# The combine stage: one row of three tiles weighted on ScalarE, four tiles normed from the residual on ScalarE and GpSimd

## The chip, the cores and the metric

The kernel runs on one core of a Trainium2 chip. Its time is the device time of one execution, in microseconds. Before the change three runs took 1245.3, 1250.42 and 1256.1 us, a median of 1250.42 us.

## The reference, cut to what matters

The program is one step of a decoder layer: a mixer, a norm, a mixture of experts, and a last norm. Only the last lines are touched here:

```python
y = lax.map(expert_block, (xb, block_e)).reshape(P, D)
out = jnp.zeros((N + 1, D), jnp.float32).at[buf_tok].add(y.astype(jnp.float32) * buf_w[:, None])
...
ff = moe(h2.reshape(B * T, D), ...)
x = layer_norm(ALPHA * x + (1 + g2) * ff, ln_g_l[1], ln_b_l[1])
```

Each token has two experts, so its `ff` is the sum of two rows of `y`, each times its weight. With r = ALPHA * x + (1 + g2) * ff, the norm is (r - mean) * rstd * ln_g + ln_b over 1024 columns. There are 1024 prompt tokens (8 tiles of 128 rows) and 64 sample tokens (tile 8, 64 rows).

## The kernel before, in words

`block_combine` is the last of the kernel's blocks. Everything in it is float32. The tiles go in order, 0 to 8, and each engine runs an order written out by hand, with semaphores between the engines.

- **GpSimd's queue** first issues 18 indirect gathers (L2759), two per tile, that fetch both expert rows of every token from the DRAM tensor `y_d` into `yy[i][0]` and `yy[i][1]`. Only then does it issue the output of tiles 0 to 7 (L2766). Such an output adds the tile to `o_y_p`, which was filled with ln_b long before, so ln_b needs no instruction in the prompt tiles.
- **ScalarE** first makes diagonal matrices of the weights for the tiles that TensorE sums (L2774), then for each tile two small scalings of the row sum (L2786, L2787), the squares with their sum (L2789) and the square root (L2792). After the statistics of tile i it scales tile i - 1 by rstd (L2780, the function `scale`), which frees its output to be sent.
- **TensorE** forms the weighted sum of both rows in PSUM (L2750) for the tiles from `ON_DVE` on, with four pairs of banks in turn.
- **VectorE** runs `residual(i)` and then `normed(i - 1)`. `residual` forms the weighted sum itself for the tiles below `ON_DVE` (L2810, L2811), multiplies by g2 (L2817) and adds ALPHA * x with the row's sum (L2821; the row's sum comes out in a short read of the accumulator). `normed` forms (r - mean) * ln_g into `nrm` (L2831) and takes the reciprocal (L2837); for the sample tile it also takes a reciprocal (L2839) and adds ln_b (L2840), after which SyncE sends it (L2859).

There are two buffers for the residual (`acc`) and three for the normed tile (`nrm`): `normed(i)` waits with `done[i % 3]` until the output of tile i - 3 has landed.

Of the kernel before, what the change touches and what calls it, by code (L numbers as in the profile page):

```python
# [26 lines left out]
ALU, ACT, AX = mybir.AluOpType, mybir.ActivationFunctionType, mybir.AxisListType  # L27
# [2683 lines left out]
def block_combine(c):  # L2711

    nc, t, sem = c.nc, c.t, c.sem
    RY = NT

    def part(n, count=1):
        return c.combine[:, D * n:D * (n + count)]

    yy = [[part(2 * s + k) for k in range(2)] for s in range(RY)]
    acc = [part(2 * RY + s) for s in range(2)]  # L2720
    nrm = [part(2 * RY + 2 + s) for s in range(3)]
    g2s = part(2 * RY + 5)
    x1 = c.raw[:, 0:NT * D].rearrange("p (i d) -> p i d", i=NT)
    lng2, lnb2, g2 = (c.raw[:, D * (NT + n):D * (NT + n + 1)] for n in range(3))
# [3 lines left out]
    st, eps, both = c.combine[:, o:o + 48], c.combine[:, o + 48:o + 49], c.combine[:, o + 49:o + 49 + NT]  # L2728
    shares = sem("y9_shares")
    diag = c.combine[:, o + 64:o + 64 + NT * 2 * P].rearrange("p (i k q) -> p i k q", i=NT, k=2)  # L2730
    n_ready, scaled, sample_out = sem("n9_ready"), sem("n9_scaled"), sem("y9_sample")
    y_in = [sem(f"y9_in{s}") for s in range(RY)]
    done = [sem(f"y9_out{s}") for s in range(3)]
    b_done, d_done, y_sum, g2_done, sum_ready, less_done, squared, var_ready, eps_set, link = (
        sem(n) for n in ("b9_done", "d9_done", "y9_sum", "g29_done", "m9_ready", "less9_done", "s9_squared", "v9_ready", "e9_set", "l9"))
    smp = NP_TILES
    ON_DVE = 2

    with nc.Block() as block:
        @block.tensor  # L2740
        def _(pe):
            for i in range(ON_DVE, NT):
                T = tile_rows(i)
                pe.wait_ge(d_done, i + 1 - ON_DVE)
                pe.wait_ge(y_in[i % RY], 32 * (i // RY + 1))
                if i >= 4 + ON_DVE:
                    pe.wait_ge(g2_done, i - 3)
                for n in range(2):
                    for k in range(2):
                        mm = pe.matmul(c.bank(2 * (i % 4) + n)[0:T, :], diag[0:T, i, k, 0:T],  # L2750
                                       yy[i % RY][k][0:T, 512 * n:512 * n + 512], start=(k == 0), stop=(k == 1))
                mm.then_inc(y_sum, 1)

        @block.gpsimd
        def _(pool):
            def fetch(i):
                T = tile_rows(i)
                for k in range(2):
                    pool.indirect_dma_start(yy[i % RY][k][0:T, :], None, c.y_d,  # L2759
                                            bass.IndirectOffsetOnAxis(ap=c.dest_y[0:T, i, k:k + 1], axis=0)).then_inc(y_in[i % RY], 16)  # L2760

            for i in range(RY):
                fetch(i)
            for i in range(smp):
                pool.wait_ge(scaled, i + 1)
                pool.dma_start(t["o_y_p"][0, i * P:(i + 1) * P, :], nrm[i % 3], accum_op=ALU.add).then_inc(done[i % 3], 16)  # L2766

        @block.scalar
        def _(act):
            act.wait_ge(shares, 1)  # L2770
            for i in range(ON_DVE, NT):
                T = tile_rows(i)
                for k in range(2):
                    a = act.activation(diag[0:T, i, k, :], c.ident[0:T, :], ACT.Identity, scale=c.xw[0:T, i, k:k + 1])  # L2774
                a.then_inc(d_done, 1)
            act.wait_ge(eps_set, 1)

            def scale(i):
                act.wait_ge(n_ready, i + 1)
                act.activation(nrm[i % 3], nrm[i % 3], ACT.Identity, scale=st[:, 24 * (i % 2) + 16:24 * (i % 2) + 17]).then_inc(scaled, 1)  # L2780

            for i in range(NT):
                T = tile_rows(i)
                q = st[0:T, 24 * (i % 2):24 * (i % 2) + 24]
                act.wait_ge(sum_ready, i + 1)
                act.activation(q[:, 8:9], q[:, 0:1], ACT.Identity, scale=-1.0 / (32 * D)).then_inc(less_done, 1)  # L2786
                act.activation(q[:, 4:5], q[:, 0:1], ACT.Identity, scale=-1.0 / D).then_inc(less_done, 1)  # L2787
                act.wait_ge(less_done, 2 * i + 1)
                act.activation(squares[0:T, :], acc[i % 2][0:T, :], ACT.Square, bias=q[:, 8:9], scale=1.0 / 32,  # L2789
                               accum_out=q[:, 12:13]).then_inc(squared, 1)  # L2790
                act.wait_ge(squared, i + 1)
                act.activation(q[:, 12:13], q[:, 12:13], ACT.Sqrt, bias=eps[0:T, :]).then_inc(var_ready, 1)  # L2792
                if i >= 1:
                    scale(i - 1)

        @block.vector
        def _(dve):
            links = [0]

            def linked(ins):  # L2800
                links[0] += 1
                ins.then_inc(link, 1)
                dve.wait_ge(link, links[0])

            def residual(i):
                T = tile_rows(i)
                ac = acc[i % 2][0:T, :]
                if i < ON_DVE:
                    dve.wait_ge(y_in[i], 32)
                    linked(dve.tensor_scalar(ac, yy[i][0][0:T, :], c.xw[0:T, i, 0:1], None, ALU.mult))  # L2810
                    linked(dve.scalar_tensor_tensor(out=ac, in0=yy[i][1][0:T, :], scalar=c.xw[0:T, i, 1:2], in1=ac,  # L2811
                                                    op0=ALU.mult, op1=ALU.add))
                    total = ac
                else:
                    dve.wait_ge(y_sum, i + 1 - ON_DVE)
                    total = c.psum[0:T, D * (i % 4):D * (i % 4) + D]
                dve.tensor_tensor(ac, total, (g2 if i < smp else g2s)[0:T, :], ALU.mult).then_inc(g2_done, 1)  # L2817
                dve.wait_ge(g2_done, i + 1)
                dve.wait_ge(c.x1_in[i], 32)
                q = st[0:T, 24 * (i % 2):24 * (i % 2) + 24]  # L2820
                dve.scalar_tensor_tensor(out=ac, in0=x1[0:T, i, :], scalar=ALPHA, in1=ac, op0=ALU.mult, op1=ALU.add,  # L2821
                                         accum_out=q[:, 0:1]).then_inc(sum_ready, 1)

            def normed(i):
                T = tile_rows(i)
                q = st[0:T, 24 * (i % 2):24 * (i % 2) + 24]
                out = nrm[i % 3][0:T, :]
                if i >= 3:
                    dve.wait_ge(done[i % 3], 16 * (i // 3))
                dve.wait_ge(less_done, 2 * i + 2)  # L2830
                linked(dve.scalar_tensor_tensor(out=out, in0=acc[i % 2][0:T, :], scalar=q[:, 4:5], in1=lng2[0:T, :],  # L2831
                                                op0=ALU.add, op1=ALU.mult))
                dve.wait_ge(var_ready, i + 1)
                if i < smp:
                    if i >= 2:
                        dve.wait_ge(scaled, i - 1)  # L2836
                    dve.reciprocal(q[:, 16:17], q[:, 12:13]).then_inc(n_ready, 1)  # L2837
                    return
                linked(dve.reciprocal(q[:, 16:17], q[:, 12:13]))  # L2839
                dve.scalar_tensor_tensor(out=out, in0=out, scalar=q[:, 16:17], in1=lnb2[0:T, :],  # L2840
                                         op0=ALU.mult, op1=ALU.add).then_inc(b_done, 1)

            dve.memset(eps, EPS).then_inc(eps_set, 1)
            linked(dve.tensor_tensor(both, c.xw[:, :, 0], c.xw[:, :, 1], ALU.add))
            linked(dve.reciprocal(both, both))
            dve.tensor_tensor(c.xw, c.xw, both.unsqueeze(2).to_broadcast([P, NT, 2]), ALU.mult).then_inc(shares, 1)
            dve.wait_ge(shares, 1)
            dve.wait_ge(c.v_in, 64)
            for i in range(NT):
                residual(i)  # L2850
                if i >= 1:
                    normed(i - 1)
            normed(smp)

        @block.sync
        def _(sp):
            sp.dma_start(g2s[0:NS, :], sample_rows(c, 5)).then_inc(c.v_in, 16)
            sp.wait_ge(b_done, 1)
            sp.dma_start(t["o_y_s"].rearrange("b j d -> (b j) d"), nrm[smp % 3][0:NS, :]).then_inc(sample_out, 16)  # L2859
            sp.wait_ge(c.out_done, c.out_total)  # L2860
            for s in range(3):
                sp.wait_ge(done[s], 16 * ((smp - s + 2) // 3))
            sp.wait_ge(sample_out, 16)
# [43 lines left out]
```

## Time and profile before

| | us |
|---|---|
| median of three runs | 1250.42 |
| the profiled execution, its own time | 1253.85 |
| its span, first to last instruction | 1252.1 |
| PE busy, share of the span | 1119.1 (89%) |
| DVE busy | 731.7 (58%) |
| ACT busy | 587.6 (47%) |
| POOL busy | 135.2 (11%) |

The span is the time from the first to the last instruction of the slowest (here the only) core; the execution's own time lies 1.75 us above it. The combine stage takes the last 58 us, from about 1194 us on. In it TensorE is not what its share in the whole kernel says: its last matmul ends near 1235 us. PE, DVE, ACT, POOL and SP are TensorE, VectorE, ScalarE, GpSimd and SyncE; a q behind the name is the engine's instruction queue, where DMA issues stand.

### The profile page before, as it was taken

Reading aid. Unit: us, or ns where it says so; the run is one execution under the profiler, and the core shown is the slowest. Engines: PE = TensorE matmul, PEld = TensorE weight load, DVE = VectorE, ACT = ScalarE, POOL = GpSimd, SP = SyncE. Lnnn points to the kernel's source line nnn. Section 1 sums busy time; section 2 is a strip of 40 time slices with the busy share of each in tenths; the row PEclk is TensorE's granted clock in tenths of the full one; section 3 lists DMA queues with packets and bytes.
Section 4 is the critical chain, followed back from the end, with each engine's and each line's share of the span. In section 5 each row is a group of like instructions: output and inputs, shape, how many; then the busy total and the mean of one; then the engine's idle time right before and its main releaser. Section 6 shows DMA issues by size and latency. Waiting matters only on the chain. (4 is left out here: it accounts for less than half of the span.)

```text
span 1252.1 us, 20501 instructions
## 1 busy us (share of the span) xinstructions
PE 1119.1 (89%) x7389; PEld 904.6 (72%) x7390; DVE 731.7 (58%) x1433; ACT 587.6 (47%) x1022; POOL 135.2 (11%) x203
## 2 busy tenths in 40 slices
PE   5699989998799999999889936999999999999844
PEld 3598879987666777778568725878888888888611
DVE  1461263243554777777676768885484588565157
ACT  0461100113465776766533235774475477555145
POOL 0212402010100000000000001020000011000061
PEclk9799999999997999999999967999999999999967
DMA  9645755054484300000343357996696599693488
GB/s 325 200 140 222 288 206 154 1 62 111 127 332 165 61 1 2 1 2 2 109 143 122 118 211 281 374 385 252 232 377 223 222 383 392 263 372 114 175 302 151
DMA packets 92343, 238.07 MB, mean 190 GB/s; under 512 B 8662, under 2 KB 18069, under 8 KB 92239
## 3 DMA queue, kind: packets, MB, share of 16 engines
q1 hardware_dynamic: 76153, 189.92, 43.2%
q0 software_dynamic: 10288, 31.20, 8.0%
q10 hardware_dynamic: 5830, 15.99, 3.6%
q8 instruction: 45, 0.74, 0.2%
q14 instruction: 27, 0.22, 0.1%
HBM read 199.04 MB, written 44.33 MB: 194 GB/s over the span
## 5 line engine op out<-in xcount | busy, mean ns | idle before, releaser
L2562 PE MATMUL psum<-w_hi,x_parts 128*128 128x512 f32 x736 | 239.7, 397 | 9.0 <-DVE x_parts L2681 9.0
L2674 DVE TENSOR_TENSOR w_lo<-raw,w_hi 128x2048 fp32r<-128x2048 f32 x95 | 213.3, 2286 | 44.7 <-ACT w_hi L2615 43.7
L2615 ACT CAST w_hi<-raw 128x2048 fp32r<-128x2048 f32 x90 | 167.6, 1914 | 29.3 <-DMA raw<-in_moe_w_gate 15.2
L2562 PEld LDWEIGHTS psum<-w_hi,x_parts 128*128 128x128 f32 x736 | 139.8, 190 | 39.8 <-issue 10.7
L2562 PE MATMUL psum<-w_lo,x_parts 128*128 128x512 f32 x368 | 144.7, 393 | 0.0
L2562 PE MATMUL psum<-w_hi,a_parts 128*128 x368 | 120.4, 399 | 4.0 <-DVE a_parts L2687 4.0
L1758 DVE CUSTOM_DVE_ANT_0 low<-psum,high 128x512 f32<-128x512 f32 (+5 forms) x172 | 92.2, 578 | 42.1 <-PE psum L1446 28.0
L1476 PE MATMUL psum<-keep,low 128*128 128x128 f32 (+1 forms) x556 | 95.0, 292 | 11.9 <-ACT high L1705 6.1
L1644 ACT ACTIVATE low<-low,high 128x640 f32<-128x640 f32 (+9 forms) x140 | 98.9, 709 | 9.9 <-DVE high L1758 9.6
L1671 ACT COPY high<-psum 128x512 f32<-128x512 f32 (+3 forms) x128 | 63.7, 502 | 81.5 <-PE psum L1476 81.3
L713 PE MATMUL psum<-h_hi,l_parts 128*128 128x384 f32 (+1 forms) x384 | 93.8, 327 | 0.0
L2037 PE MATMUL psum<-wo_parts,mix_parts 128*128 128x512 f32 x384 | 93.2, 399 | 0.0
L1476 PEld LDWEIGHTS psum<-keep,low 128*128 128x128 f32 (+1 forms) x556 | 60.9, 143 | 43.5 <-issue 28.7
L2037 PEld LDWEIGHTS psum<-wo_parts,mix_parts 128*128 128x128 f32 x384 | 72.1, 191 | 17.1 <-issue 2.1
L2562 PEld LDWEIGHTS psum<-w_hi,a_parts 128*128 128x128 f32 x368 | 69.8, 190 | 18.2 <-issue 4.2
L2562 PEld LDWEIGHTS psum<-w_lo,x_parts 128*128 128x128 f32 x368 | 69.8, 190 | 14.0
L1494 PE MATMUL psum<-high 128*64 128x128 f32 x1056 | 73.4, 283 | 0.0
L2562 PE MATMUL psum<-w_lo,a_parts 128*128 x184 | 72.2, 393 | 0.0
L713 PEld LDWEIGHTS psum<-h_hi,l_parts 128*128 128x128 f32 x384 | 67.4, 188 | 0.6 <-issue 0.4
L673 PE MATMUL psum<-l_parts,h_hi 128*128 128x384 f32 (+3 forms) x288 | 64.9, 316 | 1.5 <-DVE h_lo L941 1.3
L1446 PE MATMUL psum<-score_parts 64*128 64x512 f32 (+3 forms) x528 | 65.1, 371 | 0.0
L1494 PEld LDWEIGHTS psum<-high 128*64 128x64 f32 x1056 | 57.5, 139 | 10.4 <-issue 8.0
(384 smaller groups left out, 1734.6 us busy)
## 6 DMA issues: line engine op xcount, KB each, us to landing
raw<-in_moe_w_gate SPq DMA_DIRECT2D x16, 2048.0 KB, 11.5
raw<-in_moe_w_up SPq DMA_DIRECT2D x16, 2048.0 KB, 11.0
raw<-in_moe_w_down SPq DMA_DIRECT2D x16, 2048.0 KB, 10.8
top<-in_w_mod SPq DMA_DIRECT2D x8, 2048.0 KB, 8.0
y_d<-work ACTq DMA_DIRECT2D x24, 512.0 KB, 5.8
low<-in_w_mod SPq DMA_DIRECT2D x4, 2048.0 KB, 18.9
high<-in_x_prompt SPq DMA_DIRECT2D x16, 512.0 KB, 3.9
y_d<-high SPq DMA_DIRECT2D x1, 8192.0 KB, 23.8
```

What stands on the lines that cost most here:

```text
L673: mm = pe.matmul(stage_bank(n)[0:T, 0:WIDTHS[st]], h_parts[left][:, k, at:at + T], right[:, k, :], start=(k == 0 and left == 0 and right i ...
L713: mm = pe.matmul(piece_bank(pc)[:, 0:w], left[:, k, :], h_parts[right][:, k, toks], start=(k == 0 and left is hi and right == 0), stop=(k ...
L1446: mm = pe.matmul(c.bank(2 * g + q % 2)[:, 0:w * P], left[rows, j, :], right[rows, br, keys], start=n == 0, stop=n == 2)
L1476: mm = pe.transpose(turn_bank(what)[0:w, (k - 4 * m) * P:(k - 4 * m + 1) * P], pb[n % 3][:, g, k * P:k * P + w], c.ident)
L1494: mm = pe.matmul(c.bank(6 + br)[HD * g:HD * g + HD, j * P:(j + 1) * P], c.vs[:, k0 + k, br, g, :], pT[n % 2][:, g, k, :], start=(k == 0), ...
L1644: act.activation(x, x, ACT.Exp, bias=mx[:, at + g:at + g + 1], scale=-1.0, accum_out=sums[g]).then_inc(e_ev, 1)
L1671: act.copy(dst[:, 0:w], src[:, 0:w]).then_inc(r_act, 1)
L1758: dve.tensor_tensor_reduce(pb[n % 3][:, g, at * P:at * P + cols], c.bank(2 * g + q % 2)[:, 0:cols], bias, -1.0, least if m else 3e38, ALU. ...
L2037: mm = pe.matmul(c.bank(2 * (s % 2) + n), mixed[i % 2][l][:, k, :], wo[w][:, k, n * 512:(n + 1) * 512], start=(k == 0 and l + w == 0), sto ...
L2562: mm = pe.matmul(out, left[l][:, k * P:(k + 1) * P], w[:, bass.ds(at - o + k * step, 512)], start=n == 0, stop=n == len(steps) - 1)
L2615: act.copy(c.w_hi[:, at:at + PART // 2], c.raw[:, o:o + PART // 2]).then_inc(hi_done[p], 1)
L2674: dve.tensor_tensor(low, c.raw[:, o:o + PART // 2], c.w_hi[:, at:at + PART // 2].bitcast(F32), ALU.subtract).then_inc(c.lo_done[p], 1)
```

## The change

`ON_DVE` goes from 2 to 3, so the weighted sum of tile 2 moves from TensorE to VectorE. For tiles 0, 1 and 2 ScalarE multiplies the first row by its weight in place, and VectorE's first instruction on these tiles goes away. For tiles 4 to 7 VectorE no longer computes (r - mean) * ln_g; it computes rstd and -mean * rstd (one column each), ScalarE computes r * rstd - mean * rstd from `acc` into `nrm`, and GpSimd multiplies by ln_g ahead of the output. ScalarE waits for the landing of the buffer's earlier output in VectorE's place. VectorE waits, ahead of its first write to `acc[i % 2]` in tiles 6, 7 and 8, until ScalarE has read the tile that lay there (i - 2).

```diff
-    ON_DVE = 2
+    ON_DVE = 3
+    ON_POOL = (4, 5, 6, 7)
+    half_sum, scaled_up, pool_done = sem("y9_half"), sem("n9_on_act"), sem("n9_on_pool")
...  gpsimd
             for i in range(smp):
-                pool.wait_ge(scaled, i + 1)
+                if i in ON_POOL:
+                    pool.wait_ge(scaled_up, ON_POOL.index(i) + 1)
+                    pool.tensor_tensor(nrm[i % 3], nrm[i % 3], lng2, ALU.mult).then_inc(pool_done, 1)
+                    pool.wait_ge(pool_done, ON_POOL.index(i) + 1)
+                else:
+                    pool.wait_ge(scaled, i + 1)
                 pool.dma_start(t["o_y_p"][0, i * P:(i + 1) * P, :], nrm[i % 3], accum_op=ALU.add).then_inc(done[i % 3], 16)
...  scalar
+            for i in range(ON_DVE):
+                act.wait_ge(y_in[i], 32)
+                act.activation(yy[i][0], yy[i][0], ACT.Identity, scale=c.xw[:, i, 0:1]).then_inc(half_sum, 1)
             act.wait_ge(eps_set, 1)
 
             def scale(i):
                 act.wait_ge(n_ready, i + 1)
+                if i in ON_POOL:
+                    q = st[:, 24 * (i % 2):24 * (i % 2) + 24]
+                    if i >= 3:
+                        act.wait_ge(done[i % 3], 16 * (i // 3))
+                    act.activation(nrm[i % 3], acc[i % 2], ACT.Identity, scale=q[:, 16:17], bias=q[:, 20:21]).then_inc(scaled_up, 1)
+                    return
                 act.activation(nrm[i % 3], nrm[i % 3], ACT.Identity, scale=st[:, 24 * (i % 2) + 16:24 * (i % 2) + 17]).then_inc(scaled, 1)
...  scalar, after the loop over the tiles
+            act.wait_ge(scaled_up, len(ON_POOL))
...  vector, residual(i)
                 if i < ON_DVE:
                     dve.wait_ge(y_in[i], 32)
-                    linked(dve.tensor_scalar(ac, yy[i][0][0:T, :], c.xw[0:T, i, 0:1], None, ALU.mult))
-                    linked(dve.scalar_tensor_tensor(out=ac, in0=yy[i][1][0:T, :], scalar=c.xw[0:T, i, 1:2], in1=ac,
+                    dve.wait_ge(half_sum, i + 1)
+                    linked(dve.scalar_tensor_tensor(out=ac, in0=yy[i][1][0:T, :], scalar=c.xw[0:T, i, 1:2], in1=yy[i][0][0:T, :],
                                                     op0=ALU.mult, op1=ALU.add))
...
+                if i >= 2 and i - 2 in ON_POOL:
+                    dve.wait_ge(scaled_up, ON_POOL.index(i - 2) + 1)
                 dve.tensor_tensor(ac, total, (g2 if i < smp else g2s)[0:T, :], ALU.mult).then_inc(g2_done, 1)
...  vector, normed(i)
+                if i in ON_POOL:
+                    dve.wait_ge(less_done, 2 * i + 2)
+                    dve.wait_ge(var_ready, i + 1)
+                    linked(dve.reciprocal(q[:, 16:17], q[:, 12:13]))
+                    dve.tensor_tensor(q[:, 20:21], q[:, 4:5], q[:, 16:17], ALU.mult).then_inc(n_ready, 1)
+                    return
```

## Rows read from the trace of the kernel before

**Rows 1.** The chain of waits: start us, us, what; between the lines a repeating pattern.
```profile
1218.58 8.37 DMA out_o_y_p<-combine
...
1226.97 1.30 DVE combine L2831
...
1230.85 1.21 DVE combine L2831
```

**Rows 2.** DVE's waits from 1190 us on: engine line waited for: us in total, times, longest.
```profile
DVE combine L2831 <- DMA out_o_y_p<-combine: 2.8, 1, 2.8
DVE combine L2817 <- PE psum L2750: 1.6, 1, 1.6
```

**Rows 3.** The timeline, tiles 0 to 3: start us, us, engine line op out<-in xcount [idle].
```profile
1201.95 0.75 DVE L2810 TENSOR_SCALAR combine<-combine,keep 128x1024 f32<-128x1024 f32 x1 [7.06 <-DMA combine<-y_d,dest_y]
...
1203.82 1.02 POOL L2759 DMA_INDIRECT combine<-y_d,dest_y  x1 [0.30 <-issue]
...
1207.66 1.69 POOL L2759 DMA_INDIRECT combine<-y_d,dest_y  x1 [0.31 <-issue]
...
1214.08 1.22 DVE L2817 TENSOR_TENSOR combine<-psum,raw 128x1024 f32<-128x1024 f32 x1 [1.63 <-PE psum L2750]
```

**Rows 4.** DMA issues from 1190 us on: queue, count, KB each, median us to landing.
```profile
out_o_y_p<-combine POOLq DMA_DIRECT2D x8, 512.0 KB, 5.4
...
combine<-y_d,dest_y POOLq DMA_INDIRECT x18, 6.3
...
out_o_y_s<-combine SPq DMA_DIRECT2D x1, 256.0 KB, 5.0
```

**Rows 5.** The timeline, statistics of tile 6 and the scaling of tile 5.
```profile
1234.55 0.08 DVE L2821 DVE_READ_ACCUMULATOR combine<-raw,combine 128x1 f32 x1
1234.55 1.28 DVE L2831 SCALAR_TENSOR_TENSOR combine<-combine,raw 128x1024 f32<-128x1024 f32 x1
...
1235.94 1.21 DVE L2817 TENSOR_TENSOR combine<-psum,raw 128x1024 f32<-128x1024 f32 x1
...
1236.37 1.13 ACT L2780 ACTIVATE combine<-combine 128x1024 f32<-128x1024 f32 x1
```

**Rows 6.** The timeline, the end: tile 7's scaling and issue, the sample tile.
```profile
1242.11 0.07 DVE L2821 DVE_READ_ACCUMULATOR combine<-raw,combine 64x1 f32 x1
...
1243.72 0.29 ACT L2792 ACTIVATE combine<-combine 64x1 f32<-64x1 f32 x1
1243.92 1.13 ACT L2780 ACTIVATE combine<-combine 128x1024 f32<-128x1024 f32 x1
...
1245.35 0.86 POOL L2766 DMA_DIRECT2D out_o_y_p<-combine  x1 [2.90 <-ACT combine L2780]
1246.30 0.54 SPq L2859 DMA_DIRECT2D out_o_y_s<-combine  x1
```

**Rows 7.** GpSimd's instructions by line and shape: count | busy us, mean ns | idle.
```profile
L1621 POOL TENSOR_TENSOR low<-high 128x1024 f32<-128x1024 f32 x1 | 1.9, 1899 | 0.1
...
L2300 POOL TENSOR_TENSOR scratch<-scratch 128x144 f32<-128x144 f32 x1 | 0.5, 492 | 0.1
...
L2300 POOL TENSOR_TENSOR keep<-scratch 128x18 f32<-128x18 f32 x1 | 0.2, 218 | 0.1
```

**Rows 8.** The timeline of routing and the experts: DVE and GpSimd side by side.
```profile
744.03 0.90 POOL L2292 TENSOR_TENSOR scratch<-scratch 128x288 f32<-128x288 f32 x1 [141.26 <-DVE scratch L2329]
744.19 0.76 DVE L2355 TENSOR_TENSOR scratch<-scratch 64x16 bf16<-64x16 f32 x1
...
778.51 2.28 DVE L2674 TENSOR_TENSOR w_lo<-raw,w_hi 128x2048 fp32r<-128x2048 f32 x1
...
778.84 1.99 POOL L2538 COPY id_now<-ids_i 128x1 int32 x1 [13.98 <-PE psum L2554]
```

**Rows 9.** The timeline of attention: DVE with one input in PSUM beside GpSimd.
```profile
348.65 0.61 POOL L1627 COPY low<-high 128x512 f32<-128x512 f32 x1 [13.97 <-DVE high L1774]
...
348.89 0.42 DVE L1758 CUSTOM_DVE_ANT_0 low<-psum,high 128x256 f32<-128x256 f32 x1
```

## The prediction

> **What bounds the kernel now.** I read the chain of waits first, for what ended last. It runs through the combine stage alone: GpSimd's 18 gathers, then the output of tile 0, 8.37 us from issue to landing, which releases VectorE's L2831 at 1226.97, then VectorE without a gap to the end [rows 1]. So there are two stretches. Up to 1226.97 the end of GpSimd's gathers and that landing set the pace. Behind it VectorE does, 3.78 us per tile: two row sums lie at 1234.63 and 1242.18 [rows 5, 6], and half their distance is 3.775.
>
> VectorE's waits come second, for slack ahead of that landing. L2831 of tile 3 waited 2.8 us for an output, L2817 of tile 2 waited 1.6 us for TensorE's first sum [rows 2]. So whatever VectorE gains in tiles 0 to 2 grows the 2.8 us wait, and it may lose up to 2.8 us for nothing.
>
> The timeline comes third, for ScalarE beside VectorE. Tile 6's row sum is ready at 1234.63. ScalarE does its four statistics steps first and starts to scale tile 5 at 1236.37, 1.74 us later, for 1.13 us [rows 5]. So tile i - 1 is scaled 2.87 us after tile i's sum. Today nobody on VectorE is held by that: L2817 of tile 7 starts at 1235.94, 1.31 us after the sum, with its own L2831 between [rows 5].
>
> **The front: tiles 0 to 3.** VectorE loses two L2810 of 0.75 us and gains one weighted sum of 1.28 (the length of L2831, also two tensors and a column [rows 3, 5]). In tile 0 it waits for ScalarE, which takes 1.13 us where VectorE took 0.75: +0.4. In tile 1 it saves 0.75. In tile 2 it works 1.3 longer and the 1.63 us wait for TensorE goes: -0.3. Net 0.65 us earlier. What is late next is TensorE's sum of tile 3: its second gather was issued at 1203.82 and takes a median of 6.3 us, so it starts near 1210.1 [rows 3, 4]. Tile 2's sum took until 1214.08 from a start that the same median puts near 1207.7, so 6.4 us cold; tile 3's sum is ready near 1216.5, about where VectorE gets to it. If the gather is 2 us later, VectorE still reaches tile 3's norm before 1226.97. ScalarE's three weightings stand ahead of tile 0's statistics; the third waits for tile 2's gather (near 1207.7), so these begin near 1208.9 instead of 1206.6, and tile 0's output must only be there when GpSimd ends its gathers at 1218.58 [rows 1]. Cost: 0, under cover of the 2.8 us; with that cover gone each late us counts.
>
> The gathers' own length can change: most take 0.95 us, but 1.02 and 1.69 appear beside VectorE work [rows 3], about 1.5 us of delays over all 18. VectorE's instructions move against them, so the landing may come from 1.5 us earlier to 1.5 later. I take 0, since the same number of such instructions is met and the data still pass through the same queue.
>
> **VectorE in tiles 4 to 7.** A norm took 1.31 us of VectorE's time [rows 5]; two one-column instructions take about 0.15 each (the read of a column is 0.08, a column's root 0.29 on ScalarE [rows 5, 6]; between these ends I take 0.35 for both with their gap). That is 0.95 less, four times, 3.8 us. None of it stays, for the next wait.
>
> **The wait for ScalarE's read.** L2817 of tiles 6, 7 and 8 now waits until tile i - 2 is scaled. That is 2.87 us after the sum of tile i - 1, where L2817 used to start after 1.31. From L2817's start to the row's sum is 3.775 - 1.31 = 2.46 us. With 0.05 for the semaphore the period is 2.87 + 0.05 + 2.46 = 5.38 us instead of 3.775. The first held sum is tile 6's, counted from tile 5's, which stays at 1230.85 [rows 1]. Queued behind the wait on VectorE are the whole residual and norm, so the tail moves with it: three periods, 3 × 1.605 = 4.8 us.
>
> **GpSimd's multiply, and what it holds.** No row has this very operation. The same size with repeated inputs took 1.90 us; from the 18 and 144 column rows (0.218 and 0.492, 2.17 ns a column) 1024 columns give 2.40 us [rows 7]. The new one reads two full tensors and is near neither end more than the other: 2.15. The Trainium skill's page "GPSIMD Engine Reference", section "Elementwise — side-by-side cycle accounting", gives about 2.6 cycles an element; by its 1.2 GHz that would be an estimate of 2.2 us.
>
> It starts 0.08 us after the scaling, beside VectorE's L2817. The next, L2821, reads two tensors in SBUF. In routing, VectorE's tiny two-input L2355 took 0.76 us and ended at 744.95, where GpSimd's multiply ended (744.93); the other way, a one-column GpSimd copy took 1.99 us until VectorE's L2674 ended (778.84 + 1.99 = 780.83 against 780.79) [rows 8]. So the two block one another for a whole instruction. VectorE's L1758, with one input in PSUM, took 0.42 us inside GpSimd's copy [rows 9]; L2817 reads PSUM in tiles 6 to 8 and I let it run. L2821 would start 1.28 us after L2817's start, 4.20 after the sum; GpSimd ends at 2.95 + 2.15 = 5.10. Each held period grows by 0.90, three times, 2.7 us; with 1.90 and 2.40 us it is 2.0 and 3.5.
>
> The Trainium skill's page "SBUF — State Buffer", section "Who interferes with whom", speaks against this change: an instruction of VectorE with two SBUF inputs and a GpSimd one that reads SBUF exclude each other, one with a single SBUF input does not. By that rule L2817 runs and L2821 waits, and the trace agrees in both.
>
> **The tail.** Tile 8's sum comes at 1230.85 + 3 × 6.28 = 1249.7 (was 1242.18). Tile 7 is scaled at 1252.56. VectorE's last L2840 runs until about 3.3 us after the sum (root at 1.83 [rows 6], reciprocal, 1.28 us), to 1253.0; GpSimd waits for it, multiplies until 1255.2, and issues after some 0.5 us (from scaling to issue it was 1245.35 - 1245.05 = 0.3 [rows 6]; with its own wait between I take a little more), 1255.7. Landing takes 5.4 [rows 4]. The last landing before was the sample's, 1246.30 + 5.0 = 1251.3 [rows 4, 6], 0.8 before the span's end. So the new end is 1255.7 + 5.4 + 0.8 = 1261.9, which is **9.8 us** more. The sample output, issued at 1253.1, is no longer last. ScalarE's waits for landings hold nothing: tile 4's issue near 1236.3 lands at 1241.7, tile 7 needs it at 1251.4; VectorE's for tile 5 is met at 1248, needed at 1250.
>
> **The sum.** Wait 4.8, blocked reads 2.7, tail 2.3 (tile 7's multiply on the end), VectorE's savings nothing: 9.8. Against the profiled execution's 1253.85 it gives 1263.6. That run lies 3.4 over the median of 1250.42; from the median I forecast **1260.2 us**, 0.8% slower. About 1% is what a measurement of this kernel can tell from no change, so this is within 1%, near its edge.
>
> **The rivals.**
> 1. *No blocking* (15%). GpSimd leaves L2821 and L2840 alone: period 5.38, tile 8's sum at 1247.0, end at 1258.8, +6.7, **1257.1 us**. Rows 8 speak against it, though their instructions are small.
> 2. *The savings come through* (4%). ScalarE's order would have to put the scaling ahead of the statistics or its read not be last. Then tile 8's sum lies near 1239.2 (ScalarE's 2.87 a tile), tile 7 is multiplied by 1244.3, lands at 1250.2, and the span ends about 1 us earlier: **1249.4 us**. That little, since the multiply goes onto the end. The code's order and rows 5 speak against it.
> 3. *GpSimd's multiply is long* (17%). At 3.2 us (the 288 column row taken whole, 0.895 / 288 a column) each of three periods and the tail take 1.03 us more: +13.9, **1264.3 us**. It decides the sign from 2.9 us on, where the total passes 12.5 us. Against it: that row began beside a VectorE instruction and held delay of its own.
> 4. *GpSimd waits for L2817 too* (7%): if L2817 holds it, the multiply begins 1.2 us later, L2821 with it: +13.6, **1264.0 us**. Rows 9 speak against it.
> 5. *The first landing moves* (7%), by up to 1.5 us either way with the forecast behind it: 1258.7 to 1261.7.
>
> The rest, 50%, is the forecast. The likeliest range without a rival is 1258 to 1263. Runs of one kernel spread from 5 us under to 6 over their median, so the range of 8 in 10 is 1252 to 1267: it leaves out rival 2 and the far ends.
>
> **Chances.** Slower by over 1% (above 1262.9): rivals 3 and 4, 24% in all, mostly, and about a seventh of the rest through scatter: 0.29. Faster by over 1%: no case, 0.01 for scatter. Within 1%: 0.70.
>
> **What would show each step.** In the changed trace: L2831 of tile 3 still released by tile 0's landing near 1227, after a wait longer than 2.8; VectorE idle before L2817 of tiles 6, 7, 8, released by ScalarE, about 2.5 us, then 1.9; sums of tiles 6 to 8 spaced 6.3; L2821 in them begun or stretched by 0.9; three GpSimd multiplies near 2.15 and the last one starting at L2840's end; the chain ending in tile 7's output. The prediction is wrong if L2817 of tile 6 does not wait, if the multiplies take 1.2 or 3 us, or if the front loses more than its 2.8 us.

## The result and the profile after

The changed kernel takes **1257.62 us** against 1248.26 (medians of 17 runs each, measured side by side). The ratio is 1.0069, 95% interval 1.0053 to 1.0085: 8.6 us slower, between 6.6 and 10.6 (the two medians alone lie 9.4 apart). The forecast was 9.8 us, 1260.2 us from a median of 1250.42; the time measured is 2.6 us under it, and 2.2 of that is the base, which came to 1248.26 with more runs.

The kernel ahead of the combine stage differs by several us from one execution to the next, so profiles are compared here by the **stage**: from the start of the first gather to the end of the span. Before it is 1252.1 - 1194.89 = 57.2 us, after it 1257.3 - 1189.71 = 67.6 us. That one pair of executions says +10.4; the timed ratio says +8.6. The stage shows where time lies, the ratio how much it is.

The chain of waits of the changed kernel (start us, us, what), to be held against [rows 1]:

```profile
1211.96 9.56 DMA out_o_y_p<-combine
...
1221.55 1.29 DVE combine L2856
...
1227.16 1.23 ACT combine L2794
...
1228.49 1.24 DVE combine L2836
...
1246.62 1.23 ACT combine L2794
...
1247.92 2.56 POOL combine L2769
```

Tile 0's landing still releases the norm of tile 3 (now L2856), 31.8 us after the first gather, where it was 32.1. Behind it the chain no longer stays on VectorE: it goes in turns through ScalarE's scaling (L2794) and VectorE's residual (L2836), and ends in GpSimd's multiply of tile 7 and that tile's output. VectorE's waits tell the same (what waited for what: us in total, times, longest us), against [rows 2]:

```profile
DVE combine L2836 <- ACT combine L2794: 8.4, 3, 2.8
DVE combine L2856 <- DMA out_o_y_p<-combine: 2.8, 1, 2.8
```

The wait for TensorE is gone, the wait for the landing is still there, and three waits of 2.8 us are new (8.4 in all). One held period of the changed kernel on the timeline (start us, us, engine line op), against [rows 5]:

```profile
1225.34 0.08 DVE L2840 DVE_READ_ACCUMULATOR combine<-raw,combine 128x1 f32 x1
1225.34 0.16 DVE L2850 RECIPROCAL combine<-combine 128x1 f32<-128x1 f32 x1
...
1227.16 1.23 ACT L2794 ACTIVATE combine<-combine 128x1024 f32<-128x1024 f32 x1
1228.47 2.34 POOL L2769 TENSOR_TENSOR combine<-combine,raw 128x1024 f32<-128x1024 f32 x1 [3.11 <-ACT combine L2794]
1228.49 1.23 DVE L2836 TENSOR_TENSOR combine<-psum,raw 128x1024 f32<-128x1024 f32 x1 [2.80 <-ACT combine L2794]
1229.75 2.14 DVE L2840 SCALAR_TENSOR_TENSOR combine<-raw,combine 128x1024 f32<-128x1024 f32 x1
1231.11 0.86 POOL L2773 DMA_DIRECT2D out_o_y_p<-combine  x1 [0.30 <-POOL combine L2769]
1231.83 0.08 DVE L2840 DVE_READ_ACCUMULATOR combine<-raw,combine 128x1 f32 x1
```

The row sum of tile 5 is out at 1225.4, that of tile 6 at 1231.9: 6.49 us apart instead of 3.78. ScalarE's scaling ends at 1228.39, VectorE and GpSimd start together, and L2836, with one input in PSUM, takes its usual 1.23. L2840 takes 2.14 instead of 1.23, and it ends 1.08 us after the multiply, which is most of its own 1.23: it did its work once GpSimd was done.

The end of the stage, against [rows 6]:

```profile
1244.80 0.07 DVE L2840 DVE_READ_ACCUMULATOR combine<-raw,combine 64x1 f32 x1
...
1247.00 1.28 DVE L2865 SCALAR_TENSOR_TENSOR combine<-combine,raw 64x1024 f32<-64x1024 f32 x1
1247.92 2.56 POOL L2769 TENSOR_TENSOR combine<-combine,raw 128x1024 f32<-128x1024 f32 x1 [2.97 <-ACT combine L2794]
1248.31 0.53 SPq L2884 DMA_DIRECT2D out_o_y_s<-combine  x1
1250.78 0.87 POOL L2773 DMA_DIRECT2D out_o_y_p<-combine  x1 [0.30 <-POOL combine L2769]
```

The last multiply takes 2.56, 0.2 longer than the other three, since L2865 ran when it began.

### The profile page after: what moved, and what is told of

The parts are those of the page before. It is cut to its first block and busy times, and to the rows that moved or that the text cites. A ratio compares the mean times of both kernels' runs of the same rounds, so it can differ in the third digit from the quotient of the medians.

```text
span 1257.3 us, 20495 instructions
## 1 busy us (share of the span) xinstructions
PE 1111.3 (88%) x7381; PEld 899.0 (72%) x7382; DVE 730.6 (58%) x1432; ACT 590.4 (47%) x1023; POOL 143.1 (11%) x207
## 5 line engine op out<-in xcount | busy, mean ns | idle before, releaser
L2615 ACT CAST w_hi<-raw 128x2048 fp32r<-128x2048 f32 x90 | 167.6, 1915 | 26.0 <-DMA raw<-in_moe_w_gate 12.4
L1644 ACT ACTIVATE low<-low,high 128x640 f32<-128x640 f32 (+9 forms) x140 | 98.9, 709 | 10.9 <-DVE high L1758 10.7
L1476 PE MATMUL psum<-keep,low 128*128 128x128 f32 (+1 forms) x556 | 92.2, 286 | 12.2 <-ACT high L1705 6.1
```

Source lines behind the costliest of these rows:

```text
L1476: mm = pe.transpose(turn_bank(what)[0:w, (k - 4 * m) * P:(k - 4 * m + 1) * P], pb[n % 3][:, g, k * P:k * P + w], c.ident)
L1644: act.activation(x, x, ACT.Exp, bias=mx[:, at + g:at + g + 1], scale=-1.0, accum_out=sums[g]).then_inc(e_ev, 1)
L2615: act.copy(c.w_hi[:, at:at + PART // 2], c.raw[:, o:o + PART // 2]).then_inc(hi_done[p], 1)
```

## The experiments

The ratio is to the kernel before, with its 95% interval; the stage is of the one profiled execution. How far a stage can be trusted shows in tile 0's landing: in the ten kernels here that wait for it, it came between 30.6 us (e5) and 32.7 us (e2, e9) after the first gather, so a difference of 1 us between two stages is not more than that scatter unless a row shows where it comes from.

| kernel | stage, us | ratio |
|---|---|---|
| before | 57.2 | 1 |
| the change | 67.6 | 1.0069 (1.0053 to 1.0085) |
| e1, front alone | 1251.7 - 1194.75 = 57.0 | 1.0010 (0.9988 to 1.0032) |
| e2, tail alone | 1257.3 - 1188.70 = 68.6 | 1.0093 (1.0057 to 1.0128) |
| e3, no multiply | 1255.5 - 1192.43 = 63.1 | 1.0047 (1.0018 to 1.0076) |
| e7, two multiplies | 1263.1 - 1190.36 = 72.7 | 1.0111 (1.0065 to 1.0156) |
| e4, own residual buffers | 1248.6 - 1187.23 = 61.4 | 1.0045 (1.0025 to 1.0064) |
| e5, scaling first | 1250.2 - 1189.42 = 60.8 | 1.0059 (1.0037 to 1.0081) |
| e6, before with own output buffers | 1239.4 - 1185.11 = 54.3 | 0.9969 (0.9949 to 0.9989) |
| e8, alternate tiles, own buffers | 1246.0 - 1190.10 = 55.9 | 0.9993 (0.9967 to 1.0019) |
| e9, e4 with one tensor input | 1248.8 - 1189.10 = 59.7 | 1.0015 (0.9991 to 1.0038) |
| e10, e6 with the front | 1245.0 - 1191.53 = 53.5 | 0.9980 (0.9959 to 1.0002) |
| e11, product in PSUM | 1254.8 - 1189.82 = 65.0 | 1.0078 (1.0049 to 1.0107) |
| e12, all of it, tiles 3 and 5 | 1243.6 - 1188.09 = 55.5 | 0.9979 (0.9961 to 0.9996) |

**e1, the front alone.**

```diff
-    ON_POOL = (4, 5, 6, 7)
+    ON_POOL = ()
-            act.wait_ge(scaled_up, len(ON_POOL))
```

> The front of the change alone (ScalarE weights the first row of tiles 0 to 2, VectorE sums tile 2), with no tile given to GpSimd. Theory (tile 0's landing hides the front): L2831 of tile 3 is still released by that landing, 31.8 to 32.1 us after the first gather's start; the time is that of before, 0 +- 0.7 us. Rival (the front gives something, which is why the change measured 8.6 us and the last two stretches of its trace say 10.3): 1.5 us or more faster. Rival (the front costs): 1 us or more slower.

+1.2 us (-1.5 to +4.0), and tile 3's norm released 31.8 us after the first gather. The wait for the landing is 3.2 us here, and the stage is 0.2 under before. The time rules out a gain of over 1.5 us; it doesn't rule out a cost of 1 us, against which the stage and the release speak. By these the front is hidden, as the theory has it.

**e2, the tail alone:** `ON_DVE = 2`, VectorE weights the first row again, `ON_POOL` as in the change.

> The tail alone: tiles 4 to 7 through ScalarE and GpSimd, the front as before. Theory: the whole cost, +8.5 to +10 us over before, with three sums spaced 6.5 us. If the front of the change costs something: under +8. If the front gives 1.5 us: +10 or more.

+11.6 us (7.1 to 16.0), sums 6.49 apart. The whole cost is in the tail. The time lies over the theory's +8.5 to +10 and in the branch that gives the front a gain of 1.5 us, but its interval holds both, and e1 found no such gain. The stage is 1.0 us longer than the changed kernel's, because tile 0's landing came 32.7 us after the first gather and not 31.8. VectorE's work holds some gathers here (below), but the same ones as in the kernel before, where the landing came after 32.1: most of the difference is scatter of the landing.

**e3, the multiply left out.**

```diff
-                    pool.tensor_tensor(nrm[i % 3], nrm[i % 3], lng2, ALU.mult).then_inc(pool_done, 1)
-                    pool.wait_ge(pool_done, ON_POOL.index(i) + 1)
```

> The changed kernel with GpSimd's multiply by ln_g left out (tiles 4 to 7 of the output lack that factor); every wait of VectorE for ScalarE's read stays. Theory (two costs beside one another): L2836's wait of 2.8 us stays in tiles 6 to 8, L2840 takes its 1.23 us again, the three sums are spaced 5.44 us, tile 7 is issued 3.2 us after tile 8's sum as before: 3 x (5.44 - 3.78) = +5.0 us over before. Rival (GpSimd is the whole cost): within 1 us of before.

+5.9 us (2.2 to 9.5), which excludes the rival. VectorE's side of one period of e3:

```profile
1230.99 1.22 DVE L2834 TENSOR_TENSOR combine<-psum,raw 128x1024 f32<-128x1024 f32 x1 [2.80 <-ACT combine L2792]
1232.25 1.22 DVE L2838 SCALAR_TENSOR_TENSOR combine<-raw,combine 128x1024 f32<-128x1024 f32 x1
```

The wait of 2.80 us stays, the second instruction is back at 1.22, and the sums are 5.56 apart. So the wait for ScalarE costs 3 x (5.56 - 3.78) = 5.3 us by itself, and the multiply beside VectorE 3 x (6.49 - 5.56) = 2.8 more.

**e7, the multiply done twice**, each with its own semaphore count.

> The changed kernel with GpSimd's multiply done twice (the factor ln_g is squared in tiles 4 to 7). Theory (one instruction holds the read path, and a waiting one gets it when that ends): L2840 still waits for the first multiply only, the second waits 1.1 us for L2840; GpSimd's turn becomes about 7.2 us a tile, just over the 6.5 of the sums, and the last tile's second multiply adds its 2.4: +12 us over before. Rival (GpSimd keeps the path as long as it has work): L2840 waits for both, +2.4 us four times, +18 us.

+13.8 us (8.1 to 19.5) and sums 6.49, 7.00 and 7.01 apart: near the theory's 7.2, not the 8.9 (6.49 and another 2.4) that the rival would give. The time alone holds both +12 and +18. One period of e7:

```profile
1229.54 2.34 POOL L2769 TENSOR_TENSOR combine<-combine,raw 128x1024 f32<-128x1024 f32 x1 [3.10 <-ACT combine L2796]
...
1230.81 2.15 DVE L2842 SCALAR_TENSOR_TENSOR combine<-raw,combine 128x1024 f32<-128x1024 f32 x1
1231.95 3.21 POOL L2771 TENSOR_TENSOR combine<-combine,raw 128x1024 f32<-128x1024 f32 x1
...
1233.08 2.10 DVE L2853 TENSOR_TENSOR combine<-combine 128x1 f32<-128x1 f32 x1
```

VectorE waits for the first multiply and gets in between the two; the second then takes 3.21 and holds VectorE's product of **one column** for 2.10 us. The stage grew by 5.1 over the change's: 3.7 in the tail, which paid a second multiply and its delay, 1.0 in the periods and 0.4 in the first landing.

**e4, own buffers for the residual.** No instruction writes over a residual that ScalarE has still to read, so the wait goes.

```diff
-    acc = [part(2 * RY + s) for s in range(2)]
+    acc = [yy[s][0] for s in range(RY)]
+    spare = part(2 * RY)
...
-                if i >= 2 and i - 2 in ON_POOL:
-                    dve.wait_ge(scaled_up, ON_POOL.index(i - 2) + 1)
```

> The changed kernel with a buffer of its own for each tile's residual (the tile's first gathered row, which has been read by then), so that VectorE need not wait for ScalarE's read; the multiply stays. Theory: L2836 waits no more, but GpSimd's multiply (2.34) and L2840 (1.2) still exclude one another and GpSimd's turn with issue is 3.6 us: the sums are spaced 3.6 to 3.9 us, so VectorE's 0.95 a tile is lost there; tile 7 is issued 6.0 us after tile 8's sum instead of 3.2: +1 to +3 us over before. Rival (the wait was all there was, and the savings come through): faster than before by 0.5 us or more, sums spaced 2.9.

+5.6 us (3.1 to 8.0): neither. The wait is gone, but the sums are 2.67, 3.83 and 4.84 apart. In e4:

```profile
1229.61 2.64 POOL L2770 TENSOR_TENSOR combine<-combine,raw 128x1024 f32<-128x1024 f32 x1
...
1229.93 2.35 DVE L2850 TENSOR_TENSOR combine<-combine 128x1 f32<-128x1 f32 x1
...
1232.31 1.24 ACT L2795 ACTIVATE combine<-combine 128x1024 f32<-128x1024 f32 x1 [0.66 <-DVE combine L2850]
```

I had counted the big instruction only. VectorE's product of two single columns has two tensors in SBUF as well, is held for the whole multiply, and everything behind it on VectorE and ScalarE's next scaling with it. The sample tile's norm also waits here for a landing, 0.97 us.

**e9, that product with one tensor input.**

```diff
-  dve.tensor_tensor(q[:, 20:21], q[:, 4:5], q[:, 16:17], ALU.mult).then_inc(n_ready, 1)
+  dve.tensor_scalar(q[:, 20:21], q[:, 4:5], q[:, 16:17], None, ALU.mult).then_inc(n_ready, 1)
```

> The kernel with own residual buffers (e4) and, in place of VectorE's one-column product of two columns (L2850, 2.35 us in tile 5 where it is 0.16 alone), the same product with the one column as a scalar operand. Theory (two tensor inputs in SBUF make VectorE wait for GpSimd, whatever their size): it takes 0.2 us again, ScalarE's scaling and L2835 behind it start up to 2 us earlier, while L2839 is still held: 1 to 3 us faster than e4, the stage from the first gather to the span's end 59 to 60.5 us instead of 61.4 (before: 57.2). Rival (any VectorE instruction behind L2835 waits for GpSimd's multiply): it stays at 2 us and the time at e4's.

In e9, beside a multiply that ran until 1234.62:

```profile
1231.99 2.63 POOL L2770 TENSOR_TENSOR combine<-combine,raw 128x1024 f32<-128x1024 f32 x1
...
1232.31 0.21 DVE L2850 TENSOR_SCALAR combine<-combine 128x1 f32<-128x1 f32 x1
...
1233.68 2.04 DVE L2839 SCALAR_TENSOR_TENSOR combine<-raw,combine 64x1024 f32<-64x1024 f32 x1
```

0.21 us. The stage falls by 1.7 against e4 and the ratio to 1.0015: the theory by the row and the stage; the two intervals touch, so the time alone would not show it. L2839 is held as before (2.28 and 2.04 us). That is not the only place where VectorE's savings go. The sample tile's norm has to wait for the landing of tile 5's output, whose buffer of the three it takes, and is then held by tile 7's multiply:

```profile
1240.49 2.31 DVE L2855 SCALAR_TENSOR_TENSOR combine<-combine,raw 64x1024 f32<-64x1024 f32 x1 [4.43 <-DMA out_o_y_p<-combine]
```

And from 1228.75 on GpSimd goes from multiply to issue to multiply with gaps of 0.3 us at most, about 3.5 us a tile, until it issues tile 7's output at 1242.01. With VectorE's small product out of the way, GpSimd itself is what paces this tail.

**e5, ScalarE's order turned:** `scale(i - 1)` stands ahead of `act.wait_ge(sum_ready, i + 1)` for tiles 4 to 7, instead of behind the statistics of tile i.

> The changed kernel with ScalarE's order turned in tiles 4 to 7: it scales tile i - 1 before the statistics of tile i. Theory (ScalarE's order is the wait): scaling ends 1.65 us after the sum instead of 2.95, L2836 starts there, L2840 is still held by the multiply: sums spaced 5.3 instead of 6.5, +4 to +6 us over before. Rival (the order doesn't matter, GpSimd or the landings hold it): +8 or more.

+7.4 us (4.6 to 10.1); the stage says +3.6, which is outside that interval, and tile 0's landing, 1.5 us earlier after the first gather than before, has its part in that. The sums are 5.07 apart, near the 5.3 of the theory, and VectorE waits 1.4 us for ScalarE instead of 2.8, so ScalarE's order is half of the wait. By its time this run does not tell theory from rival.

**e6, the kernel before with own output buffers.** No norm waits for a landing any more.

```diff
-    nrm = [part(2 * RY + 2 + s) for s in range(3)]
+    nrm = [yy[s][1] for s in range(RY)]
...
-                if i >= 3:
-                    dve.wait_ge(done[i % 3], 16 * (i // 3))
```

> The kernel before with a buffer of its own for each normed tile (the tile's second gathered row), so that no norm waits for the landing of an earlier output. Theory (that landing is what hid the front): the 2.8 us wait of L2831 goes and nothing takes its place, TensorE's sums come every 3.44 us against VectorE's 3.78: 2.8 us faster. Rival (TensorE's sums or the gathers are right behind): under 1 us.

-3.9 us (-6.4 to -1.4), stage -2.9, and the 2.8 us wait is gone from VectorE's list. The landing was the bound between the two stretches. An output's median time to landing is 7.1 us here and 5.4 before.

**e10, e6 with the front of the change.**

> The front of the change (as e1) with a buffer of its own for each normed tile (as e6), so that no landing hides the front. Theory: now the front shows, 0.6 to 1 us under e6: stage 53.3 to 53.8 us (e6: 54.3, e1: 56.95), 3.3 to 4.5 us faster than before. Rival (VectorE would now wait for TensorE's sum of tile 3, a gather later than tile 2's): 54.3 or more.

Stage 53.5, 0.8 under e6, and VectorE waits for TensorE nowhere. Tile 8's row sum comes 43.53 us after the first gather and 44.18 in e6, 0.65 earlier. In time it is -2.5 us (-5.1 to +0.2), which does not separate it from e6. The trace says that the front is worth 0.8 us once nothing hides it; the time leaves that open.

**e11, the product by g2 stays in PSUM.**

```diff
-                dve.tensor_tensor(ac, total, (g2 if i < smp else g2s)[0:T, :], ALU.mult).then_inc(g2_done, 1)
+                dve.tensor_tensor(total, total, (g2 if i < smp else g2s)[0:T, :], ALU.mult).then_inc(g2_done, 1)
...
-  dve.scalar_tensor_tensor(out=ac, in0=x1[0:T, i, :], scalar=ALPHA, in1=ac, ...
+  dve.scalar_tensor_tensor(out=ac, in0=x1[0:T, i, :], scalar=ALPHA, in1=total, ...
```

> The changed kernel with the product by g2 of tiles 3 to 8 left in PSUM, so that L2840 has one input in PSUM and one in SBUF; all waits and GpSimd's multiply stay. Theory (what holds L2840 is its second SBUF input): L2840 takes 1.23 us beside the multiply, the three sums are spaced 5.45 us instead of 6.49, stage 64.4 instead of 67.6 us: +7 us over before. Rival (the multiply holds VectorE whatever it reads): spacing 6.5, stage 67 us or more.

```profile
1234.11 2.35 POOL L2769 TENSOR_TENSOR combine<-combine,raw 128x1024 f32<-128x1024 f32 x1 [2.06 <-ACT combine L2794]
...
1235.40 1.22 DVE L2840 SCALAR_TENSOR_TENSOR combine<-raw,psum 128x1024 f32<-128x1024 f32 x1
```

Beside the same multiply L2840 takes 1.22 us, and the sums are 5.56 apart as in e3, where there was no multiply. So the second SBUF input is what held it. The stage falls by 2.6; the ratio (+6.1 to +13.3 us) has too wide an interval to show that.

**e8, alternate tiles.** e4 with the output buffers of e6 and `ON_POOL = (2, 4, 6)`.

> The change with both sets of own buffers, and with only tiles 2, 4 and 6 given to ScalarE and GpSimd, so that the last tile's multiply isn't on the end. Theory: 2.8 us from the landing wait, and of 3 x 0.95 us on VectorE a part, since each multiply may hold L2840 by up to 1.1 us: 3 to 5 us faster than before. Rival (the multiply takes all that VectorE saves): 2.8 us or less.

-0.9 us (-4.1 to +2.4), stage 1.3 under before and 1.6 over e6: the rival, and more. Norms and multiplies hold one another (multiplies of 3.03, L2837 at 1.95), and tile 6's multiply held the sample's norm for 3.18 us instead of 1.27.

**e12, all of it, tiles 3 and 5 alone.**

> All of it together: the front of the change, own buffers for residuals and normed tiles, the product by g2 in PSUM, the one-column product by a scalar operand, and only tiles 3 and 5 given to ScalarE and GpSimd. Theory: no multiply beside a VectorE instruction that it holds except the norm of the next tile, which starts first; VectorE keeps both savings of 0.95: stage 51.4 to 52.2 us, 5 to 6 us faster than before, the fastest kernel here. Rival (the port still takes the savings, or TensorE's sums come too late): stage as e10, about 53.5 us.

-2.6 us (-4.9 to -0.5), stage 55.5: neither, and by its time no faster than e10. VectorE did what the theory says. From the first gather to the sample's issue it was 47.6 us in e10 (1239.16) and is 45.8 here (1233.92). But e10 ended 5.8 us after that issue and e12 9.7. e12's GpSimd, and the 16 DMA engines by stretch (us; busy of PE, PEld, DVE, ACT, POOL; TensorE's clock, DMA share, GB/s):

```profile
1223.24 1.77 POOL L2774 DMA_DIRECT2D out_o_y_p<-combine  x2 [0.30 <-POOL combine L2770]
1226.38 3.08 POOL L2770 TENSOR_TENSOR combine<-combine,raw 128x1024 f32<-128x1024 f32 x1 [1.36 <-ACT combine L2793]
1229.75 1.75 POOL L2774 DMA_DIRECT2D out_o_y_p<-combine  x2 [0.30 <-POOL combine L2770]
```

```profile
1221.00:1226.00 5.00, 5.00 (x13) 1.41 (x11) 4.89 (x9) 4.09 (x10) 3.72 (x3) 1.00 0.70 112
...
1231.00:1236.00 5.00, 0.00 (x0) 0.00 (x0) 2.79 (x5) 1.66 (x4) 1.36 (x2) 0.50 1.04 166
1236.00:1240.00 4.00, 0.00 (x0) 0.00 (x0) 0.00 (x0) 0.00 (x0) 0.00 (x0) 0.50 1.05 231
```

The outputs stand behind the multiplies on GpSimd's queue and leave in pairs; the DMA engines are idle part of the time and then full until 1240. An output's median time to landing is 8.4 us here, 6.8 in e10 and 5.4 before. Of the pair at 1223.24 the first landed in 5.2 us and the second in 9.0. The last output was issued at 1232.99, 3.2 us after the second pair began to leave, and took 9.3 us to land where e10's last took 5.4. The saving on VectorE was given back in the landing. That the multiplies on the queue are the whole reason is read from these rows; no run has e12 with outputs that leave one by one.

## Why the prediction was right, point by point

**The bound of the front**, tile 0's landing with 2.8 us of cover: right, though not in what makes the landing. The landing came 31.8 us after the first gather (32.1 before), L2856 waited 2.8 us, e1 measured no difference and e6 took the cover away for 2.9 us of the stage. In the step on the gathers I took 0 and gave 1.5 us either way. All 18 gathers of the changed kernel took 0.93 to 0.98 us, so about 1.5 us of delay went; but tile 0's output then took 9.56 us to land instead of 8.37, and 0.2 us was left. The DMA engines point to the reason. Before, from 1206 to the release at 1227, and after, from 1200 to 1222 (the columns of the last view of e12: the two numbers ahead of the last are the clock and the DMA share, the last is GB/s):

```profile
1206.00:1218.00 12.00, 10.27 (x18) 4.51 (x19) 10.16 (x15) 7.26 (x16) 9.26 (x10) 0.71 1.02 396
1218.00:1227.00 9.00, 9.00 (x22) 3.99 (x21) 6.06 (x9) 6.00 (x14) 3.37 (x4) 1.00 1.05 246
```

```profile
1200.00:1212.00 12.00, 6.89 (x13) 3.08 (x14) 11.79 (x14) 8.61 (x17) 9.26 (x11) 0.65 1.03 412
1212.00:1222.00 10.00, 10.00 (x25) 4.50 (x24) 7.07 (x11) 6.61 (x15) 2.77 (x3) 1.00 1.06 253
```

Their busy share is 1.02 to 1.06 in both, so they are full all the way, and an output that is issued earlier stands longer behind the gathers' data. That fits the row of 9.56 us; no run took data off these engines to test it. The prediction had it as one of its two reasons for taking 0. The front's own gain was smaller than the 0.65 us of the prediction: tile 3's sum came 29.05 us after the first gather instead of 29.25, and the wait for the landing was 2.79 and not longer than 2.84, so that one of its signs failed. It cost nothing, under the cover. With the cover gone, e10 against e6, the gain is 0.65.

**VectorE's savings of 3.8 us**, none of them staying: right. They lie in the three waits of 2.8 us.

**The wait for ScalarE's read**, 4.8 us: measured 5.3 in e3. The period was 5.56 instead of 5.38. Scaling from the residual with a scale and a bias took 1.23 us and not the 1.13 of scaling alone, and VectorE's start fell 0.10 us behind it instead of 0.05. This term was 0.5 us too small.

**GpSimd's multiply and what it holds**, 2.7 us: measured 2.8, the difference of the changed kernel and e3. The multiply took 2.34 us, near the upper of the two bounds (2.40, from the small shapes), and not the middle that I took. The row with repeated inputs (1.90) was the worse neighbour of an instruction that reads two full tensors. That the total is so near is partly luck: with 2.34 for the multiply the prediction's own working gives 1.09 us a period, 3.3 in all. But the held L2840 ended 1.08 us after the multiply and not a whole 1.23, which brought it back to 0.93 a period. What GpSimd holds was right as a mechanism. The Trainium skill's page "SBUF — State Buffer", section "Who interferes with whom", says that a VectorE instruction with two inputs in SBUF contends with a GpSimd one that reads SBUF, and one with a single such input does not. The runs agree on both sides: two SBUF inputs wait (2.14 in the changed kernel and, for one column, 2.35 us in e4), one does not (1.22 in e11 and 0.21 in e9).

**The tail**: from tile 8's sum to the end 12.2 us predicted, 12.4 measured (1244.9 to 1257.3), 9.9 before. The sample output landed in 2.9 us instead of 5.0, which cost nothing, as it was no longer last. Two details were off and offset one another: the last multiply did not wait for VectorE's last instruction (now L2865) but began 0.36 us before that ended, and it took 2.56 and not 2.15. Of the 2.5 us the multiply is not the whole: e3, which has none, is 10.9 us from that sum to the end, since its last output took 6.3 us to land and not 5.4.

**The sum** was 9.8. By the stage it was 10.4, in which the three terms are 5.3 + 2.8 + 2.5 and the landing's change is -0.2; the timed ratio gives 8.6 and its interval holds the forecast. The terms rest on single executions, the total on the timed runs, and 1.8 us between the two stay unassigned. Four rivals fail on a row of the changed trace: 1 (no blocking) on L2840's 2.14 us, 2 (the savings come through) on the three waits of 2.8, 3 (a multiply of 2.9 us or more) on 2.34, 4 (GpSimd waits for L2836 too) on the multiply that starts beside it at 1228.47 and takes no longer. Rival 5 moved the landing by 0.2 us. Two small slips in pricing the rivals changed no chance: by the prediction's own sum rival 4 comes to +13.4 and not +13.6, and the total passes 12.5 from a multiply of 2.83 us on, not 2.9.

What I missed lies off the changed kernel's path: I priced the two one-column instructions by their length and did not see that one of them has two SBUF inputs. In the changed kernel it runs when GpSimd is idle in all four tiles (0.16 us each). In e4, where the wait is gone, it is the next thing to be late.

## What to carry to other kernels

Handing an instruction to an idle engine makes its old owner wait for the new one if they share a buffer and the new one comes to it late: write down, from the last row that both need, when the new reader is done, and compare that with when the old owner comes back (here 2.9 us against 1.3). GpSimd is no free engine beside VectorE. In these runs a float32 VectorE instruction with two tensors in SBUF, even of one column (2.35 us), waited until GpSimd's multiply was over, and the multiply waited for VectorE in turn (3.21 us instead of 2.34 in e7). An input in PSUM (1.22 us) or a scalar operand (0.21 us) avoided it. Before an engine's work is shortened, look for a landing that hides it; here a buffer per tile gave more (2.9 us of the stage) than any shift of work between engines.

## What the runs showed that I had not expected

VectorE's work lengthens GpSimd's indirect gathers: 0.95 us alone, 1.69 before, 1.85 at most in e11. In the changed kernel VectorE's instructions of 1.25 us and the gathers, one every 1.25 us, fell into step, and not one was held. That is a matter of the execution and not of the change: e3 and e5 show it too, but the other eight kernels with the same front had one gather of 1.47 to 1.85 us each.

The adding outputs load the DMA engines fully (a share of 1.04 and 1.05) at 166 to 231 GB/s in e12: of two that leave together the second lands late (9.0 us instead of 5.2), and two that wait for a multiply do leave together. In e12 the end came 3.9 us later behind the sample's issue than in e10, more than the 1.8 us that VectorE had gained.
